# A two-model transformer step: which fences TensorE waits at, and the order of three branch sums

## The reference, cut to what matters

```python
h = rms_norm(x, g_mix[l]); z = h @ w_in[l]
y_a = chunk_relpos_attention(...)      # 256 wide: tiles 0, 1 of y
y_b = indexer_sparse_attention(...)    # 256 wide: tiles 2, 3, keys by top-k of a score
y_c = rglru_branch(...)                # 512 wide: tiles 4 to 7, a linear recurrence
merged = (gates[:, :, 0] * (y_a @ wb[:A_WIDTH])
          + gates[:, :, 1] * (y_b @ wb[A_WIDTH:A_WIDTH + B_WIDTH])
          + gates[:, :, 2] * (y_c @ wb[A_WIDTH + B_WIDTH:]))
x = x + merged @ w_out[l]
gu = rms_norm(x, g_ffn[l]) @ w_ffn_in[l]
x = x + (silu(g_) * u_) @ w_ffn_out[l]
# second block, even layer: x = x + gate * (cat(ya, yb) * silu(g) @ w_out), odd layer likewise
```

## Time and profile before

| | us |
|---|---|
| median of 3 runs | 4141.89 (4137.16 to 4143.73) |
| profiled execution | 4143.85 |
| its span | 4142.0 |
| TensorE busy | 3646.8 (88%) |
| VectorE busy | 2171.8 (52%) |
| ScalarE busy | 1415.1 (34%) |
| mean granted clock of TensorE | 0.927 of full |

### The profile page before, as it was taken

The page is one execution under the profiler, slowest core; times in us unless marked ns, Lnnn a source line. Parts: engine busy times, 40 slices in busy tenths (PEclk is TensorE's granted clock), DMA queues, the critical chain, the costliest instruction groups (busy, mean ns, idle before and its releaser), DMA issues. The chain is left out here.

```text
span 4142.0 us, 46440 instructions
## 1 busy us (share of the span) xinstructions
PE 3646.8 (88%) x19222; PEld 3017.1 (73%) x19222; DVE 2171.8 (52%) x3943; ACT 1415.1 (34%) x2519; POOL 238.0 (6%) x343
## 2 busy tenths in 40 slices
PE   7999988886999999999898788888698888888788
PEld 5888866765778888788666576776586777776667
DVE  4599934555733322323555545555535656425563
ACT  3211344444122211112344434444424445424341
POOL 2012110000100000000000000000000000000000
PEclk9799999887999999999899998988798999989999
DMA  3223330002421111111210001000211000100112
GB/s 122 83 104 126 117 108 27 21 21 81 163 82 46 46 38 51 53 47 36 87 34 23 29 26 32 26 27 22 91 61 65 31 30 30 36 20 18 32 33 95
DMA packets 69572, 230.08 MB, mean 56 GB/s; under 512 B 8745, under 2 KB 12841, under 8 KB 69361
## 3 DMA queue, kind: packets, MB, share of 16 engines
q1 hardware_dynamic: 43056, 132.68, 9.8%
q0 software_dynamic: 22848, 81.85, 5.8%
q10 hardware_dynamic: 3456, 12.58, 0.8%
HBM read 180.42 MB, written 36.17 MB: 52 GB/s over the span
## 5 line engine op out<-in xcount | busy, mean ns | idle before, releaser
L2388 PE MATMUL PS<-m,m 128*128 128x512 f32 (+3 forms) x3560 | 1419.7, 400 | 151.1 <-DVE m L2737 35.3
L2390 PE MATMUL PS<-m,m 128*128 128x512 f32 (+3 forms) x3560 | 1380.0, 389 | 0.0
L2389 PE MATMUL PS<-m,m 128*128 128x512 f32 (+3 forms) x3560 | 1379.3, 389 | 0.0
L2388 PEld LDWEIGHTS PS<-m,m 128*128 128x128 f32 (+2 forms) x3560 | 688.9, 194 | 327.5 <-issue 65.4
L2390 PEld LDWEIGHTS PS<-m,m 128*128 128x128 f32 (+2 forms) x3560 | 688.6, 194 | 137.7 <-issue 1.2
L2389 PEld LDWEIGHTS PS<-m,m 128*128 128x128 f32 (+2 forms) x3560 | 692.0, 195 | 120.2 <-issue 2.1
L2734 DVE TENSOR_TENSOR m<-m,m 128x1024 fp32r<-128x1024 f32 (+5 forms) x204 | 211.7, 1038 | 422.0 <-ACT m L2572 421.3
L3020 DVE TENSOR_TENSOR m<-PS,m 128x512 fp32r<-128x512 f32 x352 | 240.9, 689 | 295.3 <-ACT m L2664 295.0
L2664 ACT CAST m<-PS 128x512 fp32r<-128x512 f32 x352 | 205.4, 589 | 495.1 <-PE PS L2494 493.8
L2485 PE MATMUL PS<-m,m 64*128 64x256 f32 (+5 forms) x1968 | 254.1, 369 | 70.3 <-ACT m L2653 53.8
L2485 PEld LDWEIGHTS PS<-m,m 64*128 64x128 f32 (+1 forms) x1968 | 214.9, 199 | 115.0 <-ACT m L2653 69.0
(11 more groups left out here) (196 smaller groups left out, 3894.4 us busy)
## 6 DMA issues: line engine op xcount, KB each, us to landing
m<-in_w SPq DMA_DIRECT2D x220, 512.0 KB, 3.5
g_scratch<-m ACTq DMA_DIRECT2D x24, 512.0 KB, 2.6
m<-g_scratch POOLq DMA_DIRECT2D x24, 512.0 KB, 4.5
m<-in_w SPq DMA_DIRECT2D x32, 256.0 KB, 2.5
x_scratch<-m POOLq DMA_DIRECT2D x2, 4096.0 KB, 12.9
m<-m POOLq DMA_DIRECT2D x60, 128.0 KB, 2.7
m<-in_xT POOLq DMA_DIRECT2D x24, 256.0 KB, 7.4
y_scratch<-m POOLq DMA_DIRECT2D x12, 512.0 KB, 3.0
```

Source lines behind the costliest of these rows:

```text
L2388: pe.e.engine.matmul(o, L[0], X[0], start=start, stop=False)
L2389: pe.e.engine.matmul(o, L[0], X[1], start=False, stop=False)
L2390: return pe.e.engine.matmul(o, L[1], X[0], start=False, stop=stop)
```

## The change

TensorE passes seven of the eleven fences without waiting (`p.fence(False)`): the seven of the list above. The other four engines wait at all fences as before. So that TensorE stays ordered behind its inputs, three places get waits by tile: the merge's products wait for the split of the tile k that they read (`after=y_ready[k]`), the output projection for each split of the merged sums (`h_ready[d, t0] = t_m`), and `eo` for each split of y. In the merge the tiles are loaded and split in the order 4, 5, 6, 7, 0, 1, 2, 3, and the three partial products are made in the order third branch, first, second, with their gates in the same order. The number of instructions is the same on every engine.

```diff
--- before.py
+++ after.py
@@ -138,11 +138,11 @@
                 self.seen[x] = m
...
 
-    def fence(self, at):
+    def fence(self, at, wait=True):
 
...
         for name, newest in list(found.items()):
-            if name != self.name and newest is not None:
+            if wait and name != self.name and newest is not None:
                 self.wait_ge(*newest)
...
 
@@ -285,8 +285,10 @@
         self.pending.append((signal, n))
...
 
-    def fence(self):
-        self.add("fence", n=self.id(), after=list(self.pending))
+    def fence(self, pe=True):
+        self.add("fence", n=self.id(), after=list(self.pending), pe=pe)
         self.pending.clear()
...
 
@@ -1394,7 +1396,7 @@
                         modulate(nr > 18)
...
                   sink=vc("sink", 0, 8), nsink=nsink[:, :])
-            p.fence()
+            p.fence(False)
 
...
             m8 = [mem([P, 8]) for _ in range(2)]
@@ -1586,34 +1588,32 @@
         mg = mem([P, 512])
...
         g_free = [[] for _ in range(5)]
-        y_ready = []
-        for k in range(8):
-            t_d = move(gate[k % 5][:, :], y_d[k][:, 0:T], g_free[k % 5])
-            g_free[k % 5] = split(Yh[:, k, :], Yl[:, k, :], gate[k % 5][:, :], [t_d])
-            y_ready += g_free[k % 5]
-        p.add("ready", on="pe", after=y_ready)
+        y_ready = {}
+        for n, k in enumerate((4, 5, 6, 7, 0, 1, 2, 3)):
+            t_d = move(gate[n % 5][:, :], y_d[k][:, 0:T], g_free[n % 5])
+            g_free[n % 5] = y_ready[k] = split(Yh[:, k, :], Yl[:, k, :], gate[n % 5][:, :], [t_d])
         sig, t_m = [], []
...
             for c, (t0, tn) in enumerate(CH1):
-                for i, (k0, k1) in enumerate(((0, 2), (2, 4), (4, 8))):
+                for place, (i, k0, k1) in enumerate(((2, 4, 8), (0, 0, 2), (1, 2, 4))):
                     b = take()
...
                         p.add("lin", key=key, k=k - k0, L=get(k), X=(Yh[:, k, t0:t0 + tn], Yl[:, k, t0:t0 + tn]), o=bank(b),
-                              weights=event, free=bank_free[b] if k == k0 else [], after=[], last=k == k1 - 1)
-                    n = 3 * d + i
+                              weights=event, free=bank_free[b] if k == k0 else [], after=y_ready[k], last=k == k1 - 1)
+                    n = 3 * d + place
                     while len(sig) < min(n + 3, 24):
                         x = len(sig)
-                        sig.append(move(gate[(x + 3) % 5][:, :], g_d[8 * (x % 3) + x // 3], g_free[(x + 3) % 5]))
-                    p.add("merge", key=key, i=i, o=bank(b), gate=gate[(n + 3) % 5][:, t0:t0 + tn], mg=mg[:, :], t=t1b[:, :],
+                        sig.append(move(gate[(x + 3) % 5][:, :], g_d[8 * ((x + 2) % 3) + x // 3], g_free[(x + 3) % 5]))
+                    p.add("merge", key=key, place=place, o=bank(b), gate=gate[(n + 3) % 5][:, t0:t0 + tn], mg=mg[:, :], t=t1b[:, :],
                           gate_there=sig[n], free=t_m)
...
                     g_free[(n + 3) % 5] = [(S.merge, (key, "x"))]
-                t_m = split(Hh[:, d, t0:t0 + tn], Hl[:, d, t0:t0 + tn], mg[:, :], [(S.merge, ((f"wb{d}", c, 2), "sum"))])
+                t_m = split(Hh[:, d, t0:t0 + tn], Hl[:, d, t0:t0 + tn], mg[:, :], [(S.merge, ((f"wb{d}", c, 1), "sum"))])
+                h_ready[d, t0] = t_m
             release((S.lin, key))
-        p.fence()
-    h_ready = {}
+        p.fence(False)
 
...
         X = mem([P, 8, TC])
@@ -1966,7 +1966,7 @@
             assert mem.at <= z_at
...
 
-            stored, y_parts, squares_done = [], [], {}
+            stored, squares_done = [], {}
 
...
                 free = [list(ready), list(ready)]
@@ -1976,7 +1976,7 @@
                     for _ in range(4):
...
                     free[k % 2] = split(Hh[:, k, :], Hl[:, k, :], z[:, :], [t])
-                    y_parts.extend(free[k % 2])
+                    h_ready.update({(k, t0): free[k % 2] for t0, _ in CH2})
 
...
                 p.add("gsilu", n=h, z=zg[:, :], after=gate_done)
@@ -2052,8 +2052,9 @@
                 squares_done[h] = (S.norm, (units[-1]["fronts"][-1]["n"], "square"))
...
                 pass
-            y_parts += split(Hh[:, 7, :], Hl[:, 7, :], yt[:, :], y_free)
-            p.fence()
+            t = split(Hh[:, 7, :], Hl[:, 7, :], yt[:, :], y_free)
+            h_ready.update({(7, t0): t for t0, _ in CH2})
+            p.fence(False)
 
...
         X = mem([P, 8, TC])
@@ -2397,9 +2397,10 @@
             for ev in s["after"]:
...
         elif s.kind == "fence":
-            pe.fence(s["n"])
-            for ev in s["after"]:
-                pe.wait_ge(*ev)
+            pe.fence(s["n"], s["pe"])
+            if s["pe"]:
+                for ev in s["after"]:
+                    pe.wait_ge(*ev)
         elif s.kind == "ready" and s["on"] == "pe":
...
                 pe.wait_ge(*ev)
@@ -2915,13 +2916,13 @@
             key = s["key"]
...
             dve.wait_ge(*s["gate_there"])
-            if s["i"] == 0:
+            if s["place"] == 0:
                 for ev in s["free"]:
...
             else:
-                if s["i"] == 2:
-                    dve.wait_ge(S.merge, ((key[0], key[1], 1), "sum"))
+                if s["place"] == 2:
+                    dve.wait_ge(S.merge, ((key[0], key[1], 0), "sum"))
                 e.tensor_tensor(s["t"], s["o"], s["gate"], ALU.mult).then_inc(*dve.says(S.merge, (key, "x")))
```

## The result

The changed kernel takes 4104.99 us (median of 6 runs, 4091.02 to 4115.32), the kernel before beside it 4137.39 (6 runs, 4132.5 to 4143.73): a ratio of 0.992, 95% interval 0.9898 to 0.9941. 4112 with a range of 4104 to 4124 was predicted. By medians that is 32.4 us less; the profiled execution took 4107.38 us, 36.5 less than the one before. The sum of the prediction said 29.4.

A forecast was written before the change was run, and what follows sets the result against it. TensorE, busy for 88% of the span, was taken to bound the kernel. The terms -1.7 + 5.3 + 3.7 + 7.6 + 4.2 + 10.3 = 29.4 us, off the median of 4141.89, gave 4112 us, range 4104 to 4124.

The forecast's parts named there:

- A: Rival: the merge follows TensorE's start, not VectorE's pace, and keeps all 10.5 us; 4106 us in all; chance 0.08.
- B: Rival: landings of x, stores and the clock keep more across the fences; gain 17.9 us, 4124 us; chance 0.18.
- C: Rival: waits by tile end where the fences did, the first tile needed being last ready; gain 0, 4142; chance 0.04.
- Places 2, 4, 6: Fences from gates to first attention, window to differential, neighbourhood to latent attention: gains of 5.3, 7.6 and 10.3 us.
- The restart: First matmuls behind TensorE's idle time run at the lower clock, costing 1.6 to 2.6 us unless all idle time goes.
- Place 3: Fences around the merge: VectorE's 11.36 us per d sets the pace, x then delays wo2; net gain 3.7 us.
- Place 5: Fence from differential attention to projection: gain 4.2 us, capped at 4.45 by the split of the third weights.
- Place 1: Fence from scores to recurrent branch: TensorE 3.5 us ahead, then waits about 4.4; clock may fall; loss of 1.7 us.
- Rival D: In the merge, waits between short matmul groups keep TensorE at the lower clock; 4144 to 4181 us; chance 0.04.

The follow-up runs named there:

- merge_only: The changed kernel with the fences behind scores, gates, window, differential and neighbourhood attention waited at again; median 1 us more than the kernel before.
- x_tiles_before: The kernel before, with x loaded in eight whole-tile loads and no 2 MB load of second halves; worth nothing at the merge.
- x_tiles: The changed kernel, with x loaded in eight whole-tile loads and no 2 MB load of second halves; worth 12.0 us at the merge.

## Why the prediction was right, and where it was not

The mechanism held at five of the six places, and the sum of 29.4 us was 5 short of the 34.5 that the places measure. The median came out 7.0 us below 4112: 4.5 us of that is that the kernel before had a median of 4137.39 over six runs, where the prediction started from 4141.89 of three, and 2.5 us is the gain. It lies only 1 us inside the range, so with medians good to some 5 us, that it fell inside was in part luck. The range's lower end was called "between the forecast and A, 4104", though A's own value is 4106. Rivals B (17.9 us) and C (nothing) are far below what the places show.

- **Places 2, 4, 6** came out as worked: 5.4, 7.6 and 10.45 us for 5.3, 7.6 and 10.3. The idle time went, or shrank to the ScalarE copy of the bank (2357.55 + 1.54 = 2359.1, TensorE at 2359.14). The restart as a term of its own is right at place 6 (21.59 to 11.14 in every trace). At place 2 it isn't certain: with its fence waited at, merge_only took 14.91 and before 16.55, so that term is 0 to 1.6 and the place worth 3.8 to 5.4 (x_tiles_before took 16.55 again).
- **Place 3**: the step and the rival it beat were right. 11.36 us per d was found again (1044.86, 1056.22), the first merge stood at 1033.49 (1036.1 predicted, less the 3.0 us by which this trace was ahead there), the new wait was 9.5 for 11 us. The term was 3.7 and measured 4.3: x landed in 19.9 us and not 20.7.
- **Place 5**: 4.9 for 4.2, mis-sized for the same reason. The addition ahead of the eo2 weights began 20.2 us behind the first load and not 20.7, so the cap was 4.9 and not 4.45. It was there, as 0.74 us in front of eo2, and moved with x; x_tiles takes another 0.9 off.
- **Place 1 was wrong, in sign.** The step that failed is that "TensorE will be early and wait about 4.4 us there". It added the lead of 3.5 to the 0.90 us of one row, as if that row were the distance of two independent engines. It was not: VectorE had lost 2.6 us to GpSimd in that execution, and TensorE would have been the later one without it. What the runs showed in its place is a wait of 0.91 us and a gain of 2.4 us (1.9 against the one trace of before), for a wait of 4.4 and a loss of 1.7. The loss was to come from a fall of the clock, and none followed at the gate matmuls (granted 1.00 from 503 to 507 us). This is 3.6 of the 5.15 us that the sum missed; places 3 and 5 are most of the rest.
- **Rival D**: with TensorE waiting for one split after another at the start, three matmuls apart, the granted clock was 1.00 from 1025 us on:

```profile
1025.00:1032.00 7.00, 4.52 (x15) 2.14 (x14) 5.06 (x5) 4.71 (x5) 2.26 (x5) 1.00 0.98 343
...
1044.00:1108.00 64.00, 64.00 (x281) 52.49 (x281) 52.45 (x74) 11.59 (x16) 8.23 (x16) 1.00 0.52 180
```

TensorE was busy for only 4.52 of those first 7 us, and the clock held. The Trainium skill's rule on short idle times ("TensorE: Matmul & The Clock Gate", section "A second HAM failure mode: psum-queue depth-cycling"), by which the prediction had the time between 4144 and 4181, is not seen in this stage.

## What to carry to other kernels

A wait that is taken away is worth what the next late thing leaves: follow the released engine to it, name it, and then fix that (the 2 MB load of x cost 12 us only once the fence was open, and nothing before). A short wait in one trace says which engine is late in that execution and not how the two stand; before adding a lead to it, look whether an operation on either side took longer there than its equals. Where executions scatter by more than the effect, lay traces over each other by instruction number and read places, not totals.

## What the runs showed of the hardware

VectorE's one-tensor operation with a number (fp32, SBUF to SBUF) and GpSimd's subtraction exclude each other: 0.61 becomes 2.25 us, or GpSimd's 2.40 becomes 3.37. TensorE's granted clock fell behind an idle time of 2.25 us in one execution and not in another, at 1.6 us. Up to the last score matmul the traces differ by 13 us, 138.7 in x_tiles and 152.0 in merge_only. 9 us of it are there by the 100th matmul: matmuls of 128x512 go from 0.43 to 0.23 us apart near 30 us in x_tiles and near 49 us in merge_only, with the same work before.
